# Layer 2's modulation beside the experts of the third and fourth tile: ten selections to a block of weights in place of one and a half, two weight buffers in place of three

## What is computed

```python
mod_lat = silu(c) @ w_mod[l] + b_mod[l]        # w_mod[l]: 1024 x 6144; the same for c_ctx
h = rmsnorm(x, g_norm1[l]) * (1 + sc1) + sh1   # shifts, scales and gates are slices of mod
p = h @ w_in[l]                                # then attention, a short convolution and a long one by spectra
x = x + gt1 * merge(...)
h2 = rmsnorm(x, g_norm2[l]) * (1 + sc2) + sh2
# experts (PEER): per token and each of 8 heads, 16 experts of 16384 are selected by a product of keys
a = gelu(einsum('chkd,cd->chk', u_tab[e], h2))
x = x + gt2 * einsum('chk,chkd->cd', g * a, v_tab[e])
```

## Time and profile before

| what | value |
|---|---|
| median of 3 runs | 5437.69 us (5434.0 to 5438.31) |
| the profiled execution | 5433.36 us, its span 5431.3 us |
| PE / DVE / ACT / POOL busy | 69% / 61% / 37% / 37% of the span |
| granted TensorE clock, mean | 0.814 of full speed |
| gathers (queue q0) | 1342 MB of 1532 MB moved, 60.5% of 16 engines' span |
| experts of layer 0 alone, first dot to last | 1355.6 to 2668.8 us |
| modulation of layer 1 beside experts | about 2673 to 2867 us |
| layer 1's other stages beside experts | 2867 to 3586 us |

### The profile page before, as it was taken

One profiled execution on the slowest core, in us unless ns is written; L12 is line 12 of the kernel. 1 busy time (PEld: TensorE's weight loads), 2 busy tenths in 40 slices (PEclk: granted clock), 3 DMA queues, 4 the chain that ended last, 5 costly groups with the idle time before them and its releaser, 6 DMA issues. The chain is left out here.

```text
span 5431.3 us, 59703 instructions
## 1 busy us (share of the span) xinstructions
PE 3760.0 (69%) x19504; PEld 1838.0 (34%) x19504; DVE 3330.3 (61%) x7026; ACT 1988.8 (37%) x5136; POOL 2036.3 (37%) x1533
## 2 busy tenths in 40 slices
PE   6899879987565555555577679678976555555554
PEld 3677338876111111111122245246852111111111
DVE  7622452223777777777687777764135777777776
ACT  5432002212443344343354444325223443343443
POOL 5112003212444444444483356211434444444443
PEclk8999989998767777777688889889988777777777
DMA  5012002212999999999998989841327999999998
GB/s 237 16 44 70 4 16 65 63 67 103 400 418 410 416 410 417 415 414 414 378 363 349 367 327 375 349 171 37 98 80 325 421 412 417 413 415 416 411 417 345
DMA packets 230644, 1532.43 MB, mean 282 GB/s; under 512 B 26164, under 2 KB 26740, under 8 KB 58044
## 3 DMA queue, kind: packets, MB, share of 16 engines
q0 software_dynamic: 184320, 1342.26, 60.5%
q1 hardware_dynamic: 46012, 186.36, 9.4%
HBM read 1515.31 MB, written 13.21 MB: 281 GB/s over the span
## 5 line engine op out<-in xcount | busy, mean ns | idle before, releaser
L536 PE MATMUL psum<-arena 64*64 64x512 f32 x10240 | 1769.8, 825 | 1220.8 <-ACT arena L515 1209.6
L491 POOL DMA_INDIRECT arena<-in_uv,arena x1280 | 1462.9, 1143 | 1817.7 <-PE psum L536 1392.6
L651 DVE SCALAR_TENSOR_TENSOR arena<-arena 128x1024 f32<-128x1024 f32 x1280 | 1621.4, 1267 | 697.8 <-DMA arena<-in_uv,arena 653.0
L536 PEld LDWEIGHTS psum<-arena 64*64 64x64 f32 x10240 | 418.1, 169 | 2519.8 <-ACT arena L515 1892.9
L1549 PE MATMUL psum<-view_at,view_at 128*128 128x512 f32 (+1 forms) x4896 | 966.5, 359 | 19.1 <-PEq L165 10.3
L504 ACT ACTIVATE arena<-arena 128x1 f32<-128x1 f32 x1280 | 258.2, 202 | 1850.8 <-DVE arena L651 1811.0
L265 POOL TENSOR_TENSOR view_at<-view_at,view_at 128x1024 fp32r<-128x1024 f32 (+1 forms) x192 | 455.2, 2380 | 1238.7 <-ACT view_at L299 1208.4
L1549 PEld LDWEIGHTS psum<-view_at,view_at 128*128 128x128 f32 x4896 | 815.3, 191 | 185.2 <-issue 54.4
L515 ACT ACTIVATE arena<-arena 128x64 f32<-128x64 f32 x1280 | 445.1, 348 | 52.7 <-PE psum L536 10.9
L508 ACT ACTIVATE arena<-arena 128x1 f32<-128x1 f32 x1280 | 376.9, 294 | 46.7 <-ACT arena L504 0.4
L299 ACT ACTIVATE view_at<-view_at 128x1024 fp32r<-128x1024 f32 (+1 forms) x176 | 163.9, 939 | 330.6 <-DMA view_at<-in_w_in 188.2
(11 more groups left out here) (246 smaller groups left out, 3445.6 us busy)
## 6 DMA issues: line engine op xcount, KB each, us to landing
view_at<-in_w_in SPq DMA_DIRECT2D x108, 512.0 KB, 6.6
view_at<-in_w_mod SPq DMA_DIRECT2D x48, 1024.0 KB, 12.9
arena<-in_uv,arena POOLq DMA_INDIRECT x1280
view_at<-in_w_br SPq DMA_DIRECT2D x48, 256.0 KB
view_at<-in_w_out SPq DMA_DIRECT2D x16, 512.0 KB, 8.7
view_at<-in_wq SPq DMA_DIRECT2D x16, 512.0 KB, 3.4
arena<-mod_rows SPq DMA_DIRECT2D x12, 512.0 KB
keep_spectrum<-arena SPq DMA_DIRECT2D x18, 256.0 KB, 6.9
```

What stands on the lines that cost most here:

```text
L491: nc.gpsimd.indirect_dma_start(out=self.slots[i % self.ring], out_offset=None, in_=self.table, in_offset=bass.IndirectOffsetOnAxis(ap=self ...
L536: last = nc.tensor.matmul(self.c.psum[tokens, at:at + 512], self.diag[rows, k % 4], self.slots[k % self.ring][rows, D + h * 512:D + (h + 1 ...
L651: nc.vector.scalar_tensor_tensor(out=self.junk, in0=self.slots[i % self.ring][:, 0:D], scalar=1.0, in1=self.h2_turned if i % 2 else self.h ...
```

## The change

The experts run alone to 264, when `x` of tiles 0 and 1 is complete, then to 272 while those two tiles are stored. The modulation follows, beside selections 272 to 512, ten to a block, with its weights where tiles 0 and 1 had `x` (0) and normed tokens (80), and the rounded parts where they had their scores (136, 144). Then 8 selections alone, and 10 more while `x` of tiles 0 and 1 is loaded again, that of tiles 2 and 3 stored and the first filter weights loaded. The later shares begin at 530: 46, 46, 12, 82, 12 alone, 18 and 22. The fourth tile's sums move to the PSUM banks of the third and fifth, since the modulation uses banks 0 to 3. The weights have two buffers for three.

```diff
--- before.py
+++ after.py
@@ -920,16 +920,16 @@
                     in1=c.cols[:, g:g + KD].unsqueeze(2).to_broadcast([P, KD, 2]), op0=ALU.add, op1=ALU.mult).then_inc(mod_ready, 1)
 
 
-def phase_mod_beside(c, layer, lay, share, moves):
+def phase_mod_beside(c, layer, lay, share):
 
 
     nc, io = c.nc, c.io
     HALF = KD // 2
-    SLOTS = 3
+    SLOTS = 2
     n_all = 2 * (6 * D // 512)
-    raw = [c.own(136 + 8 * i, HALF * 512) for i in range(SLOTS)]
-    low = [c.rounded(136 + 8 * i, HALF * 512) for i in range(SLOTS)]
-    high = [c.rounded(at, HALF * 512) for at in (80, 88, 160)]
+    raw = [c.own(at, HALF * 512) for at in (0, 80)]
+    low = [c.rounded(at, HALF * 512) for at in (0, 80)]
+    high = [c.rounded(at, HALF * 512) for at in (136, 144)]
     rows, sel, turned_rows = c.at(189, 2, 512), c.at(184, 2), c.at(189, 2, P)
     TURNED = 3 * 512
     with Phase(nc, gathers=True) as ph:
@@ -938,7 +938,6 @@
         low_dve, low_pool, hi_ready, halves_done, kept, turned, cols_in, cond_split, dve_done = (ph.sem(s) for s in (
             "low_by_vector", "low_by_gpsimd", "high_ready", "halves_done", "rows_kept", "rows_turned", "cols_landed",
             "cond_split", "dve_steps"))
-        moved = ph.sem("moved")
 
         mod_ready, mod_turned, rows_made, rows_stored = (ph.sem(s) for s in (
             "mod_ready", "mod_turned", "rows_made", "rows_stored"))
@@ -957,9 +956,6 @@
                 if n >= SLOTS:
                     sp.wait_ge(halves_done, n - SLOTS + 1)
                 sp.dma_start(raw[n % SLOTS], io["w_mod"][layer][n]).then_inc(w_landed[n % SLOTS], 16)
-                if n < len(moves):
-                    sp.dma_start(*moves[n]).then_inc(moved, 16)
-            sp.wait_ge(moved, 16 * len(moves))
             keep_rows(sp)
 
         @ph.block.scalar
@@ -2703,7 +2699,11 @@
             sp.wait_ge(stored, 16 * NT_LAT)
 
 
-def first_stages_beside(c, layer, lay, experts, at):
+def first_stages_beside(c, layer, lay, experts):
+
+
+
+
 
     nc, io = c.nc, c.io
     keep_x = nc.dram_tensor("keep_x", (P, NT_LAT, D), F32).ap()
@@ -2711,23 +2711,29 @@
     keep_h = nc.dram_tensor("keep_h", (P, KD, L_LAT), F32).ap()
     spectra = [nc.dram_tensor(f"keep_spectrum{i}", (P, 2 * NT_LAT + 1, W_BR), F32).ap() for i in range(2)]
     x_lat, h_high = c.xs[:, 0:NT_LAT], lay.hT_high.bitcast(F32)
-    marks = list(itertools.accumulate((at, 36, 40, 40, 10, 74, 10, 18)))
-    shares = [Share(experts, a, b, n) for a, b, n in zip(marks, marks[1:], (24, 13, 13, KD + 1, 24))]
+    two, latents = 2 * experts.per_tile, NT_LAT * experts.per_tile + 8
+    marks = list(itertools.accumulate((latents + 10, 46, 46, 12, 82, 12, 18)))
+    shares = [Share(experts, a, b, n) for a, b, n in zip(marks, marks[1:], (13, 13, KD + 1, 24))]
 
     def parts(order):
         kept = spectra[order]
         return list(zip(lay.spectrum(NT_LAT, order), (kept[:, 0:NT_LAT], kept[:, NT_LAT:2 * NT_LAT], kept[:, 2 * NT_LAT])))
 
-    phase_mod_beside(c, layer, lay, shares[0], [(keep_x, x_lat)] + filter_weights(c, layer, 0))
+    phase_experts(c, experts, two + 8)
+    phase_experts(c, experts, two + 16, [(keep_x[:, 0:2], x_lat[:, 0:2])])
+    phase_mod_beside(c, layer, lay, Share(experts, two + 16, latents - 8, 24))
+    phase_experts(c, experts, latents)
+    phase_experts(c, experts, marks[0], [(x_lat[:, 0:2], keep_x[:, 0:2]), (keep_x[:, 2:4], x_lat[:, 2:4])]
+                  + filter_weights(c, layer, 0))
     for order in range(2):
-        phase_spectrum_beside(c, layer, order, lay, shares[1 + order], spectra[order])
+        phase_spectrum_beside(c, layer, order, lay, shares[order], spectra[order])
     phase_norm1_apart(c, range(NT_LAT), 0, (lay.hT, lay.hT_low, lay.hT_high), [c.xs[:, t] for t in range(NT_LAT)],
                       [c.at(at, D) for at in (124, 128)],
-                      lambda ph: SplitRing(c, ph, conv_blocks(c, layer)[:3], at=80, slots=3, high_at=189), (), shares[3])
-    phase_conv_beside(c, layer, lay, shares[4], keep_ysc, keep_x2, (keep_h, h_high))
-    phase_experts(c, experts, marks[6], [(c.at(80, 4096), io[f"dft{L_LAT}"][:, 0:4096])] + parts(0))
-    phase_long_conv(c, L_LAT, 0, lay, Share(experts, marks[6], marks[7], NT_LAT + NT_LAT // 2), parts(1))
-    phase_long_conv(c, L_LAT, 1, lay, Share(experts, marks[7], experts.n_all, NT_LAT + KB_BR), [(lay.x2T, keep_x2)])
+                      lambda ph: SplitRing(c, ph, conv_blocks(c, layer)[:3], at=80, slots=3, high_at=189), (), shares[2])
+    phase_conv_beside(c, layer, lay, shares[3], keep_ysc, keep_x2, (keep_h, h_high))
+    phase_experts(c, experts, marks[5], [(c.at(80, 4096), io[f"dft{L_LAT}"][:, 0:4096])] + parts(0))
+    phase_long_conv(c, L_LAT, 0, lay, Share(experts, marks[5], marks[6], NT_LAT + NT_LAT // 2), parts(1))
+    phase_long_conv(c, L_LAT, 1, lay, Share(experts, marks[6], experts.n_all, NT_LAT + KB_BR), [(lay.x2T, keep_x2)])
     experts.free()
     phase_norm1_apart(c, range(NT_LAT, NT), 1, (lay.hTc, lay.hTc_low, lay.hTc_high), [c.xs[:, t] for t in range(NT_LAT, NT)],
                       [c.at(at, D) for at in (112, 116)], lambda ph: qkv_ring(c, ph, layer), (4, 5), Share(),
@@ -2752,12 +2758,10 @@
         phase_merge(c, 0, lay)
         phase_out(c, 0, True, lay)
         phase_norm2(c, 0, True)
-        experts = Experts(c, 0, range(NT), (4, 0, 4, 0, 4, 4))
+        experts = Experts(c, 0, range(NT), (4, 0, 4, 4, 4, 4))
         phase_query(c, 0, True, experts)
-        latents = NT_LAT * experts.per_tile + 8
-        phase_experts(c, experts, latents)
         lay = Mixing(c, apart=True)
-        moves = first_stages_beside(c, 1, lay, experts, latents)
+        moves = first_stages_beside(c, 1, lay, experts)
         phase_qkv(c, 1, False, lay, moves)
         phase_attention(c, 1, False, lay)
         phase_merge(c, 1, lay)
```

## The result

The changed kernel takes 5482.0 us (median of 4 runs, 5476.66 to 5486.1), the kernel before on the same chip 5438.0 us (5434.0 to 5439.36). The ratio is 1.0084 [1.0072, 1.0095]: **slower by 44 us**. The forecast was 15 us faster, and the range ended at 5455. The profiled execution took 5482.83 us (span 5481.0), 49.5 more than that of before.

What follows compares the result with a forecast made beforehand. DMA bytes were taken to bound the kernel, 2.535 us a selection; -68 us up to the first spectrum and +53 in later stages gave -15, so 5418.4 profiled and 5422.7 as median, range 5396 to 5455.

Steps and rivals of the forecast that it cites:

- up to the first spectrum: All ahead of the first spectrum: 26 fewer selections -65.9, 1 MB more +2.5, idle DMA -4.6, together -68.0 us.
- norm: Norm stage: two more selections, but the tile change at 642 leaves it for the convolutions, -3 us.
- convolutions: Convolution stage: 8 more selections at 1.75 us each, 14, and 5 for the tile change moved there.
- 0.4 us a block, 9: Inside the modulation: idle DMA behind GpSimd's splits, taken as nearly covered by gathers in flight; bounds 0 and 24.5 or 47.
- rival 3: Odd modulation blocks: GpSimd's splits starve the gathers, with DVE two selections behind; 47 us for 9, total 5461; chance 0.20.
- the price of the later selections: 26 selections moved to later stages: between 0.98 us each (PE, in gaps) and 2.535 (DMA-bound); sum 53 us.
- 26 selections alone: Selections ahead of the first spectrum fall from 556 to 530, at 2.535 us each: -65.9 us.
- Two buffers: Modulation weights: each load has over 30 us against 12.9 to land, so two buffers for three cost nothing.
- The banks: Tiles 2, 3 and 4 sharing PSUM banks 4 to 7: PE's wait hidden by four gathers in flight, costed at nothing.
- The boundaries: Gaps in gather issue at barriers: 5.6 us idle each at 264 and 520, 3.6 at 272, 2.5 at 530, 5 at modulation's end.
- 38.9 removed: Idle DMA the change takes away: 5.6 us at the old boundary at 520 and 33.3 in the old modulation stage.
- The start: Modulation's start: first dot waits for the first block's landing, rounding and split while queues stay full; 3 us idle, bounds 0 and 5.6.

Runs made afterwards that it cites:

- Four ahead: Changed kernel with gathers up to 4 selections ahead instead of 3, beside the modulation only: 5441.92 us, ratio 1.0018 to the kernel before.
- five ahead: Changed kernel with gathers 5 ahead instead of 3: beside the modulation only 5421.92 us, ratio 0.9999 to the kernel before; everywhere 5405.76 us, ratio 0.9956.
- the run with 74: Changed kernel with 8 of the convolutions' 82 selections done alone behind them: 5466.08 us, ratio 1.0058 to the kernel before.

## Why the prediction was wrong

The profiled executions differ by +49.5 us where the sum said -15, a miss of 64.5. It splits as follows (stages cut at their loads, the first from the load of the keys ahead of the experts, so the column may be off by half a microsecond).

| Part | predicted | measured |
|---|---|---|
| up to the first spectrum | -68.0 | -30.0 |
| spectra | +29 | +33 |
| norm | -3 | +2.7 |
| convolutions | +19 | +29.3 |
| alone, long convolutions | +8 | +10.4 |
| the rest, unchanged code | 0 | +4.3 |

**The step that failed first** is "In flight then are four gathers less what DVE is behind, 10.1 us, and most of a weight block (2.5). So nearly covered ... I take 0.4 us a block, 9." Without the hole at its start (below) the modulation has 59.9 - 7.2 = 52.7 us of idle DMA: 44 more than taken, at a place named as rival 3, whose 47 it exceeds. The pause was summed from where ACT begins to round (1.9 + 4.7 + 0.94). But it runs from the last gather, and GpSimd waits 5.0 us in the mean for ACT, whose rounding stands in its queue behind the weights of the step before. A piece of the filters' MLP (L749 1.9 us in the mean, L752 1.6, with 0.8 behind it) follows most of the splits ahead of the gather, which the sum left out. So the pause, 11.6 us in the mean and 11.3 in the one shown, with the next issue and the way to the first bytes still to come, stands against 10.1 in flight. The 2.5 us of a weight block did not cover it: the hole shown is 4.8 us, twelve times over 58, and 52.7 is what the stage has. Four ahead gave back 34 of the 46 us and five all of it, which is what a pause that outruns its cover does.

Rival 3 had the place right and its mechanism half right: the splits starve the gathers, but not through a DVE that falls behind, since it had waited for its gathers ahead of six of the seven stretched dots. That its 47 us came near the 52.7 is chance. The dots do stretch: the rule cited from the Trainium skill (SBUF — State Buffer, Who interferes with whom) agrees with the trace in kind, as the dot that began beside the split at 2199.14 took 3.50 us and ended 1.1 after it. But with five ahead the dots stay stretched and the time is back, so the lock costs nothing here that a ratio can tell.

**The second step that failed** is the price of the later selections. Both bounds were of one selection by itself, 0.98 and 2.535 us. The 26 cost 75.4 with the tile change, or 2.9 each, above the upper bound. "Convolutions: 8 at 1.75, midway, since PE (0.88) and DMA (0.95) are both near full, 14" came to 26.6, 3.3 each (the run with 74). They did not fall into gaps. With five ahead the stage is 12.6 us shorter (280.3 to 267.7), so part of its length is gathers issued late, but the price of the added work stays (30.2 us with the tile change, at three and at five ahead). Whether it comes from PE's fixed order or from the lower granted clock stays open. In the norm, the relief expected from moving the tile change away (-3) was not there, +2.7.

**What held.** 26 selections alone are worth 66.3 (65.9 in the sum). Two buffers: one wait, at the first block. The banks: free, and one wait of PE for DVE's second read of a shared bank in the modulation stretch, 6.1 us. One more MB: the page's queue for loads and stores moved 187.40 MB, 186.36 before. The boundaries: some 4.7 us idle at 264, 6.9 at the modulation's end, 5.6 at 520, and none to be seen at 272 and 530, 17 in all where 22.3 were summed (5.6 + 3.6 + 5 + 5.6 + 2.5). With the modulation's 59.9 that makes 77 us added for 38.9 removed; -65.9 + 2.5 + 77 - 38.9 = -25, against the -30.0 of the table. The windows of the changed kernel in the holes of three of them, at the modulation's start, and at 530, where there is none:

```profile
2016.00:2020.00 4.00, 0.00 (x1) 0.00 (x0) 2.55 (x11) 0.16 (x1) 0.00 (x0) 0.93 0.31 129
...
2056.00:2060.00 4.00, 2.10 (x9) 0.63 (x13) 2.34 (x2) 2.37 (x4) 0.00 (x0) 0.50 0.24 96
2060.00:2064.00 4.00, 2.54 (x21) 0.69 (x17) 3.90 (x7) 1.92 (x8) 1.25 (x2) 0.89 0.00 0
...
2776.00:2780.00 4.00, 2.35 (x12) 0.80 (x16) 3.19 (x5) 1.30 (x5) 2.27 (x2) 0.50 0.24 59
...
2800.00:2804.00 4.00, 1.10 (x8) 0.50 (x12) 2.95 (x7) 1.56 (x6) 1.40 (x1) 0.69 0.39 76
...
2832.00:2836.00 4.00, 2.04 (x4) 0.67 (x4) 2.44 (x4) 2.04 (x3) 1.32 (x1) 0.96 1.00 416
```

The start cost 7.2 us where 3 were taken. The first block's transfers were issued from 2041.56 on, and ACT could round it only at 2055.72, 14 us later; by then the gathers had landed, and from 2056 to 2064 the DMA moved 96 and 0 GB/s.

Left open: the 4.3 us of unchanged code, one profiled run of each (4.3 shorter ahead of the experts, 8.5 longer behind the long convolutions); the first block loaded ahead of the phase, and GpSimd's split cut in two halves with a gather between, which were not tried.

## What to carry to other kernels

A queue that issues transfers and also computes has a pause, and it is measured from the last issue before the work to the first issue after it, the waits for others and every small piece in between included; compare that with what is in flight, and if the difference is small, take the case where it fails as the likeliest. Look-ahead is a setting of each stage: here, with ten gathers to a block, two more of them won 46 us, and with one and a half to a block the same two lost 22, because they waited for slots ahead of work that others needed. And do not price an item added to a stage whose engines are both near full between the two bounds of the item by itself: here it cost 3.3 us, where it costs 0.98 on PE and 2.5 alone.

## What was not expected of the hardware

A block of 1 MB, issued with a second behind it while the gathers kept the DMA full (413 GB/s), took 14 us to land; ahead of it were the gathers in flight and four small loads. The rate came back in steps behind the pause shown (88, 289, 367, then 418 GB/s in 4 us each), so a hole costs more than the time in which nothing moves. And the dots beside a GpSimd split, 3.50 us in place of 1.23, were no loss that a run could tell in a stretch that goes by its transfers.
